# Rolling two transformer layers into one hardware loop, with x_lo on GpSimd and two small transposes moved ahead

## The reference

```python
DEPTH = 2; D_MODEL = 1024; SEQ = 256; D_FF = 2816
def swiglu(x, w_gate, w_up, w_down):
    return (jax.nn.silu(x @ w_gate) * (x @ w_up)) @ w_down

def first_block(x, ...):
    for l in range(DEPTH):
        x = layer_norm(ALPHA * x + 0.5 * swiglu(x, ffn1_w_gate[l], ffn1_w_up[l], ffn1_w_down[l]), ln1_g[l], ln1_b[l])
        y = hybrid_mixer(x, w_in[l], b_gate[l], pool_w[l], pool_scale[l], cmp_pos_k[l], cmp_k_w1[l], ...)
        x = layer_norm(ALPHA * x + y, ln2_g[l], ln2_b[l])
        x = layer_norm(ALPHA * x + 0.5 * swiglu(x, ffn2_w_gate[l], ffn2_w_up[l], ffn2_w_down[l]), ln3_g[l], ln3_b[l])
    return x

def compress(kv, pos, w1, w2):          # inside hybrid_mixer, once for keys, once for values
    ...
    flat = (blocks + pos).reshape(B, G, S // CMP_STRIDE - 1, CMP_BLOCK * dh)
    return jax.nn.gelu(flat @ w1) @ w2
```

## Time and profile before

| | |
|---|---|
| median of 3 runs | 2525.82 us (2522.77 to 2525.98) |
| profiled execution: its time | 2525.82 us |
| profiled execution: span from first to last instruction | 2524.0 us |
| mean granted TensorE clock | 0.951 of full speed |
| busy share of the span | PE 92%, VectorE 57%, ScalarE 44%, GpSimd 3% |
| first block, from the first swiglu to the end of layer 1 | about 23 us to 1200 us of the span |

### The profile page before, as it was taken

The page is one execution under the profiler, slowest core; times in us unless marked ns, Lnnn a source line. Parts: engine busy times, 40 slices in busy tenths (PEclk is TensorE's granted clock), DMA queues, the critical chain, the costliest instruction groups (busy, mean ns, idle before and its releaser), DMA issues. The chain is left out here.

```text
span 2524.0 us, 37919 instructions
## 1 busy us (share of the span) xinstructions
PE 2317.8 (92%) x14468; PEld 1914.7 (76%) x14468; DVE 1448.4 (57%) x2366; ACT 1127.2 (45%) x1907; POOL 86.5 (3%) x117
## 2 busy tenths in 40 slices
PE   7999989999999998999769997869999989986998
PEld 6877977887887877887447886648888777865886
DVE  6664247566665326666554666374554554436886
ACT  3443245444443235444366665343343444535654
POOL 0000000000000000000001222000000000000000
PEclk9999989999999979999899998989999979988999
DMA  8886125785886413883112110134333343304662
GB/s 233 261 263 198 36 84 174 254 262 160 252 266 206 108 67 110 252 265 123 52 41 76 46 66 2 34 117 125 107 117 117 117 117 84 93 1 131 202 184 91
DMA packets 389794, 346.82 MB, mean 137 GB/s; under 512 B 24244, under 2 KB 353320, under 8 KB 389160
## 3 DMA queue, kind: packets, MB, share of 16 engines
q1 hardware_dynamic: 379588, 294.46, 39.6%
q10 hardware_dynamic: 10084, 50.66, 5.1%
HBM read 344.03 MB, written 1.05 MB: 137 GB/s over the span
## 5 line engine op out<-in xcount | busy, mean ns | idle before, releaser
L555 PE MATMUL ps<-x_hi_lo,gu_hi 128*128 128x512 f32 x1680 | 423.5, 394 | 2.4 <-DVE gu_sum L717 2.4
L555 PEld LDWEIGHTS ps<-x_hi_lo,gu_hi 128*128 128x128 f32 x1680 | 305.7, 188 | 81.6 <-issue 19.3
L717 DVE TENSOR_REDUCE gu_sum<-ps 128x256 f32<-128x512 f32 x220 | 150.4, 689 | 245.6 <-PE ps L557 243.5
L632 ACT ACTIVATE gu_hi<-w_gu 128x1024 fp32r<-128x1024 f32 x220 | 228.9, 1054 | 111.1 <-DVE gu_sum L717 48.6
L700 DVE TENSOR_TENSOR gu_lo<-w_gu,gu_hi 128x1024 fp32r<-128x1024 f32 x220 | 260.7, 1219 | 15.0 <-ACT gu_hi L632 14.7
L557 PEld LDWEIGHTS ps<-x_hi_lo,gu_lo 128*128 128x128 f32 x1680 | 228.8, 190 | 16.8
L557 PE MATMUL ps<-x_hi_lo,gu_lo 128*128 128x256 f32 x1680 | 233.8, 282 | 0.0
L584 PE MATMUL ps<-dn_hi,h_hi 128*128 128x512 f32 x440 | 173.5, 394 | 3.0 <-DVE h_lo L742 3.0
L584 PE MATMUL ps<-dn_lo,h_hi 128*128 128x512 f32 x440 | 172.9, 393 | 0.0
L584 PE MATMUL ps<-dn_hi,h_lo 128*128 128x512 f32 x440 | 171.9, 391 | 0.0
L643 ACT ACTIVATE silu<-gu_sum 128x256 f32<-128x256 f32 x88 | 36.7, 417 | 266.9 <-DVE gu_sum L717 266.9
(11 more groups left out here) (413 smaller groups left out, 4913.3 us busy)
## 6 DMA issues: line engine op xcount, KB each, us to landing
w_gu<-in_ffn_w_up SPq DMA_DIRECT2D x176, 512.0 KB, 6.4
w_dn<-in_ffn_w_down SPq DMA_DIRECT2D x132, 512.0 KB, 3.5
w_mod<-in_w_mod ACTq DMA_DIRECT2D x64, 768.0 KB, 6.9
w_gu<-in_ffn_w_gate SPq DMA_DIRECT2D x88, 512.0 KB, 5.2
odd_w<-in_odd_w_qkv SPq DMA_DIRECT2D x24, 512.0 KB, 5.3
w_gu<-in_ffn_w_down SPq DMA_DIRECT2D x11, 1024.0 KB, 4.9
hgrn_w<-in_even_w_in SPq DMA_DIRECT2D x20, 512.0 KB, 3.8
wo<-in_w_out SPq DMA_DIRECT2D x2, 4096.0 KB, 13.2
```

The source lines that it names most:

```text
L555: pe.matmul(gu(a), gu_hi[n][:, a, f, :], x_both[:, f, :, :], start=(f == 0), stop=False, skip_group_check=True)
L632: act.activation(gu_hi[n][:, a, :, :], wgu[n][:, a, :, :], ACT.Copy).then_inc(s["w_hi"], 1)
L717: dve.reduce_sum(c[n][:, a, :], gu(a).rearrange("p h t -> p t h"), AX.X).then_inc(s["c_ready"], 1)
```

## The change

It has four parts. (1) The Python loop over layers becomes a hardware loop, `nc.Fori(0, DEPTH)`: one copy of the five phases, run twice, in which the layer number l is in a register. Addresses of weights in HBM and of layer norm parameters in SBUF are then computed by register instructions. The last phase loads the first tiles of `ffn1` for layer `l * -1 + 1` in both rounds, so in the second round as well, where nothing uses them. `settle` moves into the loop. (2) x_lo is computed by GpSimd. (3) dn_lo of tiles 0 and 1 is made ahead of step 0. (4) The two transposes of `pos_rows` stand ahead of the token products.

```diff
@@ ffn_phase
             @block.gpsimd
             def _(pool):
+                for f in range(FT):
+                    pool.wait_ge(s["x_hi"], f + 1)
+                    pool.tensor_tensor(x_lo[:, f, :], src(f), x_hi[:, f, :].bitcast(F32), ALU.subtract).then_inc(s["x_lo"], 1)
                 if mod:
                     pool.tensor_copy(cst[:, :], k.c_pad[:, 0, :]).then_inc(s["c_staged"], 1)
...
-                    if fixed == 0:
-                        lo_dn(0, 5)
                     if conv is not None:
...
-                    if fixed == 0:
-                        lo_dn(1, 6)
                     if mod and fixed == NF - 2:
...
                 for n in range(2):
                     lo_gu(n, 0, 2 * n + 1, first=(n == 0))
                     lo_gu(n, 1, 2 * n + 2)
-                    if n == 0:
-                        dve.wait_ge(s["x_hi"], FT)
-                        for f in range(FT):
-                            dve.tensor_tensor(x_lo[:, f, :], src(f), x_hi[:, f, :].bitcast(F32), ALU.subtract).then_inc(s["x_lo"], 1)
+                for n in range(2):
+                    lo_dn(n, n + 5)
                 tiles(dve, step, lambda f, first: None)
@@ mixer1_project, TensorE
+                pe.wait_ge(s["pos_in"], 32)
+                for n in range(2):
+                    last = pe.transpose(k.ps[0:HD, 7, n * CBLK:(n + 1) * CBLK], pos_rows[:, n, :], k.ident[0:CBLK, 0:CBLK])
+                last.then_inc(s["pos_turned"], 1)
+
                 for tt in range(TT):
...
-                pe.wait_ge(s["pos_in"], 32)
-                for n in range(2):
-                    last = pe.transpose(k.ps[0:HD, 7, n * CBLK:(n + 1) * CBLK], pos_rows[:, n, :], k.ident[0:CBLK, 0:CBLK])
-                last.then_inc(s["pos_turned"], 1)
@@ build
-        for l in range(DEPTH):
-            def norm(n, l=l):
+        with nc.Fori(0, DEPTH) as l:
+            def norm(n):
...
-                m.w_tok = inner.enter_context(nc.sbuf_tensor(f"w_in_tok_{l}", [P, FT, 256 + 2 * KVW + 3 * NH], F32))
-                m.w_keys = inner.enter_context(nc.sbuf_tensor(f"w_in_keys_{l}", [P, FT, 4 * KVW], F32))
+                m.w_tok = inner.enter_context(nc.sbuf_tensor("w_in_tok", [P, FT, 256 + 2 * KVW + 3 * NH], F32))
+                m.w_keys = inner.enter_context(nc.sbuf_tensor("w_in_keys", [P, FT, 4 * KVW], F32))
...
             ffn_phase(nc, k, *ffn_weights(2, l), x, ln=norm(3), mod=mod_part(l, 2), loaded=tiles,
-                      ahead=first_loads(tiles, *ffn_weights(1, l + 1)) if l + 1 < DEPTH else (), reloads=l + 1 < DEPTH)
-        settle(nc)
+                      ahead=first_loads(tiles, *ffn_weights(1, l * -1 + 1)), reloads=True)
+            settle(nc)
```

## The result

The changed kernel took 2557.74 us, the kernel before 2525.9 us beside it: the ratio is 1.0126, 95% interval [1.0108, 1.0143], so 31.8 us longer. The forecast was 2536.4 us, and its range ended at 2548: the direction was right, the size wrong by 21 us.

What follows compares the result with a forecast made beforehand. The prediction took TensorE, busy 92% of the span, as the bound. Its terms, 5.5 + 0.6 + 3.0 + 1.6 - 0.4 - 0.5 + 0.8 = +10.6 us, on 2525.8 gave 2536.4 us, range 2529 to 2548.

Steps and rivals of the forecast that it cites:

- Transposes: Start of the projection, both layers: TensorE waits for the pos_rows load, 2.77 us later each time, +5.5 us in all.
- layer norms: Six layer norms: computed addresses for scale and shift cost 0.14 us each, the others hidden; +0.8 us.
- Loop's end: Border between the layers: a second barrier with settle, +0.6 us, and the jump back over a layer, 3 us.
- The settle: Border between the layers: a second barrier comes in, VectorE idle 0.93 us against 0.31, +0.6 us.
- The jump: Border between the layers: engines branch back and must get their code again, 3 us, bounds nothing to 9 us.
- Start of layer 1's first swiglu: ScalarE's table load and register instructions delay gu_hi and so VectorE's first reduction; +1.6 us.
- x_lo on GpSimd, dn_lo early: VectorE's chain 0.4 us shorter: -0.4 us over second swiglus, -0.5 in the second block's last feed-forward; GpSimd's work hidden.
- The sign it named: Profile after, second swiglus: TensorE's wait for gu_sum would be about 0.2 us.
- C: Rival: engines that jumped back fetch again at each phase border, 23 us at ten borders; 2556 us, chance 0.12.
- A: Rival: pieces cost next to nothing, jump free, clock rises at the same moment as now; 2530.0 us, chance 0.15.
- B: Rival: early dn_lo frees buffers, gu_sum and h_lo waits vanish, jump free, pos_rows lands in time; 2520.4 us, chance 0.04.

Runs made afterwards that it cites:

- e13: Kernel before with x_lo on GpSimd, released one by one, and both dn_lo ahead of the first tile; Python loop, late transposes: ratio 1.0057, 2540.64 us.
- e12: Kernel before with ffn_both_phase's GpSimd subtractions moved to VectorE, and fewer, wider casts and x_lo subtractions in the swiglu phases: ratio 0.9983, 2521.19 us.
- e9: Kernel before with a settle between the two layers of the Python loop, nothing jumping back: ratio 1.0003.
- e1: Kernel before with the hardware loop over the two layers alone, barrier and settle inside it: ratio 1.0034, about +8.6 us.
- e14: Kernel before with the hardware loop and the early transposes, x_lo and dn_lo as before: ratio 1.0063, 2544.08 us.
- e8: Kernel before with both dn_lo splits ahead of the first tile and nothing else: ratio 1.0045, +11.4 us.
- e3: Kernel before with the two transposes of pos_rows ahead of the token products, nothing else: ratio 1.0037, +9 us.
- e2: Kernel before with the eight x_lo subtractions of each swiglu phase on GpSimd, released by one x_hi each: ratio 1.0053, +13 us.

## Why the prediction was wrong, step by step

- *Transposes, +5.5 forecast; layer norms, +0.8.* Right in kind, and in size partly by luck. Measured +3.4 and +2.1 with the layer norm ahead of each in it, and 0.3 for each of two more: 6.1 against 6.3. The wait on the load is the one named. But two sizes in it were off and cancel: with a computed address the second load is issued 0.87 us behind the first in layer 0 and 0.56 in layer 1, where it was 0.38 and 0.14 were added for the address; and it is there 1.8 us after its issue (237.79 to 239.62), not 2.3. That the clock stays low behind it (0.50 from 238 to 241 in the changed kernel) was named too.
- *Loop's end, +3.6 forecast.* Right in kind: the border took 4.7, so 1.1 were missing. The settle was priced well (0.6, measured 0.5). The jump took about 4 where 3.0 was taken, within 0 to 9. The 1.2 at the block's end are also there in `e13` (1.2) and `e12` (1.2), which have no loop, and not in `e9`: they are not shown to be the loop's, and what they hang on stays open.
- *Start of layer 1's first swiglu, +1.6.* Right in kind: `e1` and `e14` have 2.4 and 2.6. In the changed kernel it doesn't come on top: this start grew by 3.0 us in all, less than the 3.6 that x_lo and dn_lo cost there without a loop (`e13`).
- *x_lo on GpSimd, dn_lo early: -0.4 and -0.5, and 0 in layer 0.* This is the step that failed. The prediction took VectorE's chain to be eight subtractions shorter and two dn_lo longer, which `e8` confirms for dn_lo, and asked of GpSimd only whether it would be done in time. It was. What it never asked, and so put at nothing, is what GpSimd's work does to VectorE while both run: casts +3.25 and gu_lo +1.0 us in each phase. The net of 0.4 us shorter became 3.8 longer. The sign it named, a wait of about 0.2 us for gu_sum in the second swiglus, came out at 2.11 and 2.10. Five phases with 3.8 us would be 19; the starts took 15.9 (the first hides part behind TensorE's start at the low clock), and 3.9 more were lost inside three phases. In two of these a stretch behind the wait is at the lower clock (0.53 from 39 to 42, and next section); for the third, in the last feed-forward, the cause is open. Forecast for all this, with the layer's start, was +0.7; measured 19.8. That is 19 of the 21 us.
- *The rivals.* C gave 2556, nearly the time, by a mechanism that `e1` refutes: the loop alone costs 8.6 us, not the 26 that C has for it (23 for fetches, 0.6, 1.6 and 0.8). A number met by the wrong cause is no hit. A fell: the jump isn't free, and the clock didn't rise at the same moment as before but was still at 0.50 from 238 to 241, in `e3` too. B fell: the jump isn't free and TensorE does wait for `pos_rows`.
- *The row was at hand.* The earlier trace rows has GpSimd's L988 as a price for GpSimd. The partner's row in the same trace, L1042 with casts between 411 and 1500 ns (shown above), would have shown a cast waiting out a subtraction of 1.4 us.

## What to carry to other kernels

When work moves to an idle engine, price what it does to the neighbour it runs beside, not only its own length: look in the trace for a place where the two already overlap and compare min with max of one form. In these runs the fp32 casts on VectorE did not overlap with either kind of work on GpSimd, subtractions or memsets; the two-input subtractions suffered beside a GpSimd that reads, and not beside memsets. And a chain that feeds a wait of 0.44 us has no room: an instruction of 2.35 us put ahead of the reduction costs its whole length, though its result is wanted anyway.

## What the runs showed that I had not expected

A wait of 2 to 3 us on TensorE can cost more than itself, but doesn't always. In the changed kernel, behind the wait of 2.10 us in the second swiglu of layer 1, eight products take 3.11 us, and the stretch they lie in has the clock at 0.55:

```profile
1027.55 3.11 PE L555 MATMUL ps<-x_hi_lo,gu_hi 128*128 128x512 f32 x8 [2.10 <-DVE gu_sum L720]
```

```profile
1028.00:1031.00 3.00, 3.00 (x11) 2.45 (x10) 2.14 (x3) 2.31 (x3) 0.00 (x0) 0.55 1.08 344
```

The same wait in layer 0 (2.11 us, above) had no such effect: 2.08 us. And the same code at the same place starts at either level in different executions. The stretch of the earlier trace rows, at 0.50 and 0.73 there, in `e2`, where nothing in this phase was changed:

```profile
232.00:235.00 3.00, 1.41 (x4) 0.87 (x5) 2.26 (x6) 2.52 (x8) 0.31 (x1) 1.00 0.04 10
235.00:238.00 3.00, 3.00 (x9) 1.52 (x8) 2.25 (x7) 3.00 (x6) 0.00 (x0) 1.00 0.46 99
```

The projection is 2.7 us shorter there; it is 1.8 us shorter in `e9`, too, whose edit comes later. So single profiled executions differ by about 2 us at such a start, and terms below that are to be taken from several kernels or from rows that don't hang on the clock, such as VectorE's. What decides the level there is open.
